# A hybrid decoder layer on one core: another order of work ahead of the decode units, and a first up tile made from x times the gains of the norm

## The reference

```python
h = rms_norm(x, norm1_g) * (1 + scale1) + shift1       # shifts, scales, gates: silu(c) @ w_ada, per sequence
x_lru, g_lru, q_lat, kv_lat, k_rope = split(h @ w_in)
lru_out = rg_lru(causal_dwconv(x_lru)) * gelu(g_lru)   # scan over the tokens
q = rms_norm(q_lat) @ w_uq                             # 8 heads, 64 + 32 wide; norms per head, rotation
attn = attend(q, rms_norm(kv_lat), rotated k_rope)     # keys and values are kv_lat @ w_ukv
x = x + gate1 * (concat(rms_norm(lru_out), rms_norm(attn)) @ w_o)
h2 = rms_norm(x, norm2_g) * (1 + scale2) + shift2
val, gt = split(causal_dwconv(h2 @ w_up), 2)           # width 3, 2 x 2816 columns
x = x + gate2 * ((gelu(gt) * val) @ w_down)
```

## Time and profile before

| | |
|---|---|
| median of 3 runs | 946.93 us (945.82 to 947.53) |
| the profiled execution | 949.23 us, its span 947.4 us |
| PE busy | 919.8 us, 97% of the span, 7805 matmuls |
| DVE, ACT, POOL busy | 637.4, 513.1, 184.3 us |
| chain that ended last | PE 88%, DVE 6%, ACT 2%, DMA 2% |
| DMA | 106 GB/s in the mean |
| longest waits of PE | 5.7 us for x_sample, 3.2 for w_ada, 2.4 for normed_low (L2392), 1.6 for xT |
| PE in front of stored_columns | 1.0 us, for ACT's copy of the fourth stored row (L1620) |

### The profile page before, as it was taken

How to read it: one execution, slowest core, us unless ns; L and a number is a source line. 1 busy time by engine, 2 the same in 40 slices (tenths; PEclk the granted TensorE clock), 3 DMA queues, 4 the chain that set the end, 5 groups by cost and what they waited for, 6 DMA issues and landing times.

```text
span 947.4 us, 20112 instructions
## 1 busy us (share of the span) xinstructions
PE 919.8 (97%) x7805; PEld 858.7 (91%) x7805; DVE 637.4 (67%) x1241; ACT 513.1 (54%) x1147; POOL 184.3 (19%) x163
## 2 busy tenths in 40 slices
PE   5899999999999999999999989999999999999998
PEld 3588876799999999999899979999999999999997
DVE  2893378488888888888863667777777777722321
ACT  2414845689889889898863354444444443311111
POOL 0032323333333324333330301100000001000000
PEclk9999999999999999999998999999999999999999
DMA  9996732300212203202130423333333331653202
GB/s 338 332 281 222 223 134 102 146 2 23 91 59 77 90 24 112 90 24 90 46 91 23 113 60 90 89 89 90 92 96 98 97 97 50 161 153 80 63 1 91
DMA packets 107897, 100.12 MB, mean 106 GB/s; under 512 B 7125, under 2 KB 96597, under 8 KB 105770
## 3 DMA queue, kind: packets, MB, share of 16 engines
q1 hardware_dynamic: 104030, 77.91, 28.1%
q0 software_dynamic: 3456, 20.97, 6.2%
q10 hardware_dynamic: 340, 0.27, 0.1%
HBM read 96.41 MB, written 2.94 MB: 105 GB/s over the span
## 4 chain that ended last, share of the span: by engine, by line
PE 88%; DVE 6%; ACT 2%; DMA 2%; issue 1%; SPq 0%; POOL 0%; DVEq 0%; ACTq 0%; POOLq 0%
PE ps L890 51%; PE ps L1286 20%; PE ps L885 6%; PE ps L1247 2%; PE ps L1183 2%; PE ps L923 2%; DMA RW<-w_ada 2%; PE ps L1062 1%; PE ps L896 1%; PE ps L1282 1%; DVE RB L1996 1%; PE ps L1209 1%; DVE input_low L1929 1%; DVE up_weights_low L2371 0%; DVE small L1970 0%
## 5 line engine op out<-in xcount | busy, mean ns | idle before, releaser
L890 PE MATMUL ps<-normed_high,up_weights_high 128*128 128x260 f32 x704 | 142.5, 284 | 2.5 <-DVE normed_low L2392 2.4
L890 PE MATMUL ps<-normed_high,up_weights_low 128*128 128x260 f32 x704 | 142.5, 284 | 0.0
L890 PE MATMUL ps<-normed_low,up_weights_high 128*128 128x260 f32 x704 | 142.1, 284 | 0.0
L1791 ACT ACTIVATE up_weights_high<-RW 128x1024 fp32r<-128x1024 f32 x44 | 46.6, 1061 | 128.0 <-PE ps L890 128.0
L836 POOL TENSOR_TENSOR latents_low<-RB,latents_high 128x512 fp32r<-128x512 f32 x64 | 82.7, 1292 | 165.7 <-ACT latents_high L1667 165.6
L1286 PE MATMUL ps<-key_weights_high,latents_high 128*128 128x260 f32 x512 | 113.3, 302 | 0.1
L890 PEld LDWEIGHTS ps<-normed_high,up_weights_high 128*128 128x128 f32 x704 | 108.9, 189 | 3.1 <-issue 2.2
L890 PEld LDWEIGHTS ps<-normed_high,up_weights_low 128*128 128x128 f32 x704 | 109.1, 189 | 0.0
L890 PEld LDWEIGHTS ps<-normed_low,up_weights_high 128*128 128x128 f32 x704 | 108.7, 189 | 0.0
L1286 PE MATMUL ps<-key_weights_high,latents_low 128*128 128x260 f32 x512 | 103.1, 283 | 0.0
L1286 PE MATMUL ps<-key_weights_low,latents_high 128*128 128x260 f32 x512 | 103.1, 283 | 0.0
(11 more groups left out here) (350 smaller groups left out, 2069.5 us busy)
## 6 DMA issues: line engine op xcount, KB each, us to landing
RW<-w_ada SPq DMA_DIRECT2D x24, 1024.0 KB, 7.0
RW<-w_up SPq DMA_DIRECT2D x44, 512.0 KB, 5.1
RW<-w_down SPq DMA_DIRECT2D x8, 1408.0 KB, 7.3
RW<-w_in SPq DMA_DIRECT2D x11, 512.0 KB, 6.4
RB<-w_o SPq DMA_DIRECT2D x8, 512.0 KB, 4.2
RB<-x_prompt SPq DMA_DIRECT2D x2, 1024.0 KB, 12.2
o_y_p<-RB SPq DMA_DIRECT2D x4, 448.0 KB
cst<-consts SPq DMA_DIRECT2D x1, 844.5 KB, 12.0
```

The lines of the kernel that those rows point to most:

```text
L890: last = mm(ps[j % 4][rows[0]:rows[1], h, 0:H], lhsT, src[:, h * H:(h + 1) * H], start=start, stop=stop)
L1791: A(wuH[:, KT * g:KT * g + KT, :], wup[:, c, KT * g:KT * g + KT, :], ACT.Copy).then_inc(s_whi, 1)
```

## The change

Stage A. Both orders of jobs change. GELU's tile w_in(11) moves ahead of queries(3). The product with GELU's result and the modulation's last rows move ahead of query tile 3 in DVE's stream, and the modulation's last columns behind it. The recurrent norm (squares, sum, root, lru_normed, split_queries) moves ahead. POOL makes the low key weights and issues the gathers of step 1 behind its additions. Seven calls of `keep_busy` go.

Stage B. The first two up tiles, (0, 0) and (0, 1), are made from x times gains, without root and shift: the decode columns in the same way, and 12 more columns hold the shifts themselves, so that the products give W'(g x) and W'shift. Behind the product DVE multiplies by the root and ACT adds the shift. The tiles from (1, 0) on use h2 as before, which now goes through a ring of five tiles. The sum of the norm stands inside the first tile's products. The state of the convolution is fetched ahead of the last tiles and turned before tile 6 of the output projection.

```diff
@@ jobs
-               "q2", "q3", "w11", "kv0", "kv1"])
-PREP_ORDER = [("c5", 3), ("qst", 3), ("kv2", 1), ("qa", 3), ("kv3", 2), ("spread", 0), ("l0", 3), ("l1", 0), ("l2", 3), ("l3", 0),
-              ("nlru", 1), ("l4", 3), ("l5", 0), ("l6", 3)]
+               "q2", "w11", "q3", "kv0", "kv1"])
+PREP_ORDER = [("c5", 3), ("qst", 3), ("nlru", 3), ("kv2", 1), ("qa", 3), ("kv3", 2), ("spread", 0), ("l0", 3), ("l1", 0),
+              ("l2", 3), ("l3", 0), ("l4", 3), ("l5", 0), ("l6", 3)]
-J_N2, J_FST = job(9), job(10)
+J_N2, J_FST = job(19), job(15)
...
+XW = T + 12
+XH = XW // 2
+HR = 5
@@ sync
-            full(sp, J_WO[KT - 1])
             sp.dma_start(fs_tok, t["state_ffn_conv"].rearrange("l b r (m c) -> (l r m) b c", c=P)).then_inc(s_fst, 16)
@@ gpsimd
-            full(pool, J_WIN[7])
-            nc.gpsimd.memset(QBD[:, :, :, :], 0.0).then_inc(s_bdz, 1)
+            pool.wait_ge(s_kw, 2)
+            for e in range(2):
+                nc.gpsimd.tensor_tensor(kwL[:, e, :, 0:4 * NOPE], wkn[:, :].rearrange("p (g n) -> p g n", g=2),
+                                        kwH[:, e, :, 0:4 * NOPE].bitcast(F32), ALU.subtract).then_inc(s_kw, 1)
...
-            for n in range(2):
-                cached_keys(n, n)
-                cached_latents(n, n)
-
+            cached_keys(0, 0)
+            cached_latents(0, 0)
+            nc.gpsimd.memset(QBD[:, :, :, :], 0.0).then_inc(s_bdz, 1)
             for k in range(1, LT):
...
+            cached_keys(1, 1)
+            cached_latents(1, 1)
@@ tensor, stage A
             queries(2)
-            queries(3)
             w_in(11)
             later_chunk(15)
+            queries(3)
             pe.wait_ge(s_kvn, 1)
             keys_and_values(0)
...
+            claim(pe, J_NLRU)
+            pe.wait_ge(s_lrn, LT - 1)
+            both(J_NLRU, ones, lru_sq[:, 0, :], True, True).then_inc(psum_full[J_NLRU % 4], 1)
             keys_and_values(2)
...
-            keep_busy(spare, 3)
             pe.wait_ge(s_kr, 2)
-            for a in range(4):
+            for a in range(5):
                 stored_rows(a)
-                keep_busy(spare, 1)
-            claim(pe, J_NLRU)
...
@@ tensor, stage B
             for m in range(4, KT):
+                if m == 6:
+                    claim(pe, J_FST)
+                    pe.wait_ge(s_fst, 16)
...
-            keep_busy(flat(j)[:, 768:1024], 4)
...
+            def first_products(g, k):
+                j = up_job(g)
+                for n, (w, x) in enumerate(((wuH, x_high[k]), (wuH, x_low[k]), (wuL, x_high[k]))):
+                    for h in range(2):
+                        last = mm(ps[j % 4][:, h, 0:XH], w[:, KT * g + k, :], x[:, h * XH:(h + 1) * XH],
+                                  start=(k == 0 and n == 0), stop=(k == KT - 1 and n == 2))
...
+            for k in range(KT):
+                pe.wait_ge(s_xlo, k + 1)
+                if k in (0, 4, KT - 1):
+                    pe.wait_ge(s_xs, 1 + (0, 4, KT - 1).index(k))
+                first_products(0, k)
+                if k == 1:
+                    claim(pe, J_N2)
+                    pe.wait_ge(s_nsum, KT - 2)
+                    both(J_N2, ones, sq[:, 0, :], True, False)
+                if k == 2:
+                    pe.wait_ge(s_sq, 2 * KT + 12)
+                    both(J_N2, ones, sq[:, KT - 1, :], False, True).then_inc(psum_full[J_N2 % 4], 1)
...
@@ scalar
+            prep_squares(J_Q[3], query_sq, HEADS * QK)
+            act.wait_ge(s_lrud, 2)
+            lru_squares(0)
+            prep_rstd(4, 2 * HEADS)
+            lru_squares(2)
             key_squares(0)
             key_squares(1)
-            act.wait_ge(s_lrud, 2)
-            lru_squares(0)
             prep_rstd(5, HEADS)
-            lru_squares(2)
             prep_rstd(6, HEADS)
+            rstd(J_NLRU, LW).then_inc(s_rs, 1)
...
+                A(x_high[k][:, 0:NP], xT[:, k, 0:NP], ACT.Identity, bias=small[:, 1:2], scale=gmod[:, k, 0:1]).then_inc(s_xhi, 1)
...
+                if k < KT - 1:
+                    act.wait_ge(s_xused, k + 1)
+                else:
+                    full(act, up_job(1))
+                A(hH[:, k, :], h2[:, k % HR, :], ACT.Identity, bias=modT[:, 3 * KT + k, 0:1]).then_inc(s_h, 1)
@@ vector, stage A
             mod_columns(4)
-            for a in range(2, 4):
-                prep_sums(1 + a, query_sq, HEADS)
-                prep_query_tile(a)
+            prep_sums(3, query_sq, HEADS)
+            prep_query_tile(2)
+            mod_rows(5)
+            dve.wait_ge(s_g, 1)
+            V.tensor_tensor(GG[:, :, :], TA[:, :, :], GG[:, :, :], MUL).then_inc(s_lrud, 1)
+            prep_sums(4, query_sq, HEADS)
+            prep_query_tile(3)
...
-            mod_rows(5)
             mod_columns(5)
-            dve.wait_ge(s_g, 1)
-            V.tensor_tensor(GG[:, :, :], TA[:, :, :], GG[:, :, :], MUL).then_inc(s_lrud, 1)
             full(dve, J_QST)
...
             key_sums(2)
+            dve.wait_ge(psum_free[J_QA % 4], free_value(J_QA))
+            split_queries(0)
+            dve.wait_ge(s_rs, 5)
+            lru_normed()
             full(dve, J_SPREAD)
@@ vector, stage B
+            def gained_low(k):
+                dve.wait_ge(s_xhi, k + 1)
+                V.scalar_tensor_tensor(x_low[k][:, 0:NP], xT[:, k, 0:NP], gmod[:, k, 0:1], x_high[k][:, 0:NP].bitcast(F32), MUL, SUB).then_inc(s_xlo, 1)
+            def gained_samples(a, b):
...
             for m in range(KT):
                 residual(J_WO[m], m, 2 * KT, s_x1, m + 1)
                 if m + 4 < KT:
                     out_low(m + 4)
+                if m > 0:
+                    gained_low(m - 1)
                 if m == 4:
+                    gained_samples(0, 4)
                     up_low(0, 0, 1)
                     up_low(0, 1, 2)
+                if m == 5:
+                    full(dve, J_FST)
...
+                if m == 6:
+                    gained_samples(4, KT - 1)
+            gained_samples(KT - 1, KT)
+            gained_low(KT - 1)
...
+            for k in range(HR):
+                scaled_samples(k)
+                scaled(k)
+                if k == 2:
+                    first_scaled(0)
+                    up_low(1, 0, 3)
+            for k in range(KT):
+                normed_low(k)
+                if 0 < k <= KT - HR:
+                    dve.wait_ge(s_hlo, KT + k)
+                    scaled_samples(k - 1 + HR)
+                    scaled(k - 1 + HR)
+            first_scaled(1)
```

More of the change, by code:

```diff
@@ L261 @@
 J_WO = [job(n) for n in (0, 1, 2, 11, 4, 5, 6, 8)]
-J_N2, J_FST = job(9), job(10)
[L263 to L268, removed]
-def up_job(n):
-    return job(UP0 + n)
+J_N2, J_FST = job(19), job(15)
+BY_MLP = [n + m for n, m in zip(USED, (3, 2, 2, 5))]
+def up_job(n):
+    slot = (n + 1) % 4
+    return slot + 4 * (BY_MLP[slot] + n // 4)
+DOWN0 = 2 * FT
+J_FT = up_job(DOWN0 + 2)
+J_DOWN = [up_job(DOWN0 + m + (m >= 2)) for m in range(KT)]
+J_Y = [up_job(DOWN0 + KT + n) for n in (1, 2, 3, 5)]
+J_YL, J_YS = up_job(DOWN0 + KT + 4), up_job(DOWN0 + KT + 6)
+XW = T + 12
+XH = XW // 2
+HR = 5
 def build(nc, t):
@@ L549, in build @@
         s_x1 = sem("x1_done")
+        s_xhi = sem("gained_high")
+        s_xlo = sem("gained_low")
+        s_xs = sem("gained_samples")
+        s_xused = sem("gained_used")
+        s_first = sem("first_up_scaled")
         s_wup = [sem(f"w_up_in{e}") for e in range(2)]
@@ L1377, in _ @@
             for m in range(4, KT):
+                if m == 6:
+                    claim(pe, J_FST)
+                    pe.wait_ge(s_fst, 16)
+                    for b in range(NS):
+                        c = 512 * (b // 4) + 4 * FT * (b % 4)
+                        last = tr(flat(J_FST)[:, c:c + 4 * FT], fs_tok[:, b, :], 4 * FT)
+                    last.then_inc(psum_full[J_FST % 4], 1)
                 claim(pe, J_WO[m])
@@ L1381, in _ @@
                     out_products(m, k)
-            claim(pe, J_N2)
-            pe.wait_ge(s_nsum, KT - 2)
-            both(J_N2, ones, sq[:, 0, :], True, False)
-            pe.wait_ge(s_sq, 2 * KT + 12)
-            both(J_N2, ones, sq[:, KT - 1, :], False, True).then_inc(psum_full[J_N2 % 4], 1)
-            j = J_FST
-            claim(pe, j)
-            keep_busy(flat(j)[:, 768:1024], 4)
-            pe.wait_ge(s_fst, 16)
-            for b in range(NS):
-                c = 512 * (b // 4) + 4 * FT * (b % 4)
-                last = tr(flat(j)[:, c:c + 4 * FT], fs_tok[:, b, :], 4 * FT)
-            last.then_inc(psum_full[j % 4], 1)
             def up_products(e, g, k):
@@ L1641, in _ @@
                 stored_rows(a)
-            rstd(J_NLRU, LW).then_inc(s_rs, 1)
             stored_rows(4)
@@ L1832, in mlp @@
                     down_high(0)
-                evacuate(m, i, e, 1)
+                first_evacuate(1) if isinstance(i, int) and m == 0 else evacuate(m, i, e, 1)
                 if left >= 2:
@@ L1841, in _ @@
             up_high(1, 0, 1, up_job(0))
-            evacuate(0, 0, 0, 0)
```

(26 more changed lines are left out.)

133 lines of the change are left out of this document (73 added, 60 removed).

## The result

| | before | after |
|---|---|---|
| median | 947.53 us (5 runs, 945.82 to 949.82) | 954.42 us (5 runs, 953.00 to 956.69) |
| ratio, 95% interval | | 1.0075 [1.0057, 1.0093] |
| the profiled execution | 949.23 us, span 947.4 | 956.69 us, span 954.9 |
| queries(2) to unit 0 | 144.78 to 182.19: 37.4 us | 145.39 to 191.09: 45.7 us |
| unit 0 to the copy that waits for up tile five (ACT, L1791 before, L1826 after) | 182.19 to 584.43: 402.2 us | 191.09 to 591.98: 400.9 us |

The loss is 7.1 us by the ratio, predicted were 3.3 with a range that ended at 953.5. By the profiles it is +8.3 in stage A and -1.35 in stage B, and 0.6 us that lie ahead of queries(2). Behind the fifth up tile the two traces run alike (363.0 and 362.9 us to the end).

What follows compares the result with a forecast made beforehand. TensorE, busy 97% of the span, was taken as the bound. Stage A +5.3 (order +3.1, clock +1.0 and +1.2) and stage B -2.0 gave +3.3 us: 950.2 us from a median of 946.93, range 944.5 to 953.5.

Steps and rivals of the forecast that it cites:

- steps 1 to 6: Ahead of unit 0: the new queue order makes TensorE wait 6.3 us for J_QST's slot; unit 0 at 185.3, +3.1 us.
- Step 7: Ahead of unit 0: TensorE's clock falls twice, 3.4 us at 1.2 GHz each, costing +1.0 and +1.2 us.
- The upper bound: Stage A, ahead of the decode units: at most +7 us, around a forecast of +5.3.
- Stage B (-2.0): Entrance of the MLP: 4.6 us won at the second up tile, of which 2.0 remain by tile five.
- the open 10.6 us: Entrance of the MLP before the change: first two up tiles ended at 567.1 instead of 556.5; 1.7 of it clock.
- the idle row: Sign of being right: TensorE idle some 5 to 6 us in front of the turning of the sample queries.
- the clock: Sign of being right: TensorE's granted clock at 0.5 after the idle row ahead of the units.
- the last residual: Sign of being right, at the MLP's entrance: VectorE's last residual ready near 551.
- Unit 0 "near 186 to 188": Sign of being right: the first decode unit starts near 186 to 188.
- draw: Rival, 25%: port waits and second clock fall stay out; A +2, B -3, total 946 to 948.8.
- Faster: Rival, 15%: VectorE reaches mod_columns(5) before TensorE wants J_QST; no 6.3 us wait, A -3.2, B -2, about 941.7.
- The last one: Rival, 5%: state's DMA lands past 536.5 and clock falls in first up tile; B +0.5, A as forecast, 953.

Runs made afterwards that it cites:

- all fillers: Changed kernel plus 13, 3 and 4 filler calls in TensorE's three idle stretches ahead of the units: 952.71 us, ratio 1.0047 against the kernel before.
- experiment 5: Stage B's diff with state copies on ScalarE, ratio 0.9992; kernel before repeated unedited, 0.9980; kernel before plus four filler calls at the MLP's entrance, 0.9997.
- experiment 6: Changed kernel with stage A's queues reordered and state copies on ScalarE: ratio 1.0001; the same with four filler calls between stored rows: 0.9999.
- stage B alone: Only the diff's stage B parts, put on the kernel before: 947.20 us, ratio 1.0001.
- stage A alone: Only the diff's stage A parts, put on the kernel before: 956.09 us, ratio 1.0102.
- additions held back: Changed kernel with GpSimd's additions of the recurrent squares held until VectorE's last query tile is done: 952.84 us, one run.
- columns copied early: Changed kernel with VectorE copying the modulation's last columns right behind the product with GELU's result, ahead of the last query tile: 954.43 us, ratio 1.0073.

## Why the prediction was right in its order and wrong in its size

**Stage A, steps 1 to 6 (order, +3.1): right.** The wait was predicted as 6.3 us up to 166.9; measured are 6.13 up to 167.45, of which 0.6 lie ahead of queries(2). Slot, port waits (2.3 predicted, 2.0 measured) and VectorE's order were the cause; with the clock held up the order costs 3.5 us. The wait in front of the second stored row, 177.7 less the norm's end in my working, is there with 1.89 us.

**Step 7 (clock, +1.0 and +1.2): this step failed.** I took the length that the trace of before shows at both stages, 3.4 us at 1.2 GHz, for each of the two falls. Measured are 10.2 and 6.8 us, and 4.8 us of time instead of 2.2: 2.8 for the first fall instead of 1.0, 1.95 for the second instead of 1.2. Nor did VectorE hide 0.7 us of the first, as the step has it. In the timelines of DVE, the changed kernel first and the one with all fillers behind it, VectorE itself waits for J_QA:

```profile
176.69 0.27 DVE L2219 COPY QA<-ps 128x64 f32<-128x64 f32 x1 [4.45 <-PE ps L1156]
```
```profile
174.62 0.28 DVE L2223 COPY QA<-ps 128x64 f32<-128x64 f32 x1 [1.83 <-PE ps L1158]
```

The upper bound ("+7" for the whole stage, measured +8.3) rested on the same length, although the idle stretch in front was ten times that of before (6.13 against 0.60 us). The trace of before held a longer fall, the 6.8 us near 500 (0.66 in the stretch of experiment 5). Half of that for each of two falls gives 3.1 + 3.4 + 3.4 = +9.9 as an estimate of the upper bound, and that would have held. Why one fall is long and another short, no run here shows. The Trainium skill (TensorE: Matmul & The Clock Gate, "HAM oscillation — how this bites in real kernels") names waits between bursts as what throttles the array again. The first fall, in 6.13 us of idle, agrees. The second came with a wait of 1.89 us and thin rows, the kernel before without fillers fell for 10.2 us behind waits of 0.60 and 0.32 us, and experiment 6 shows that equal waits needn't give equal falls: that the rule would give both falls, as the prediction has it, isn't borne out as it stands there.

**Stage B (-2.0): right in its steps, smaller at its end.** Less the 8.9 us of stage A, with the prediction behind it: the state's wait 1.46 (1.5), the factor 554.8 (554.4), the second tile 562.85 (562.5), the start of tile four 570.8 behind the low weights (570.5), its end 576.9 (576.4). The gain of 1.85 us at tile four is 1.35 at tile five. The wait for low weights of 0.17 us in front of tile five is a part of that; the rest I can't name. That 1.7 of the open 10.6 us were the clock was wrong: with and without that fall the first five tiles take the same time. In the ratio stage B alone shows +0.1 us, -0.9 to +1.2; its profile's -1.2 lies just outside, while two equal kernels came out 0.9 us apart by their medians and 0.2% by the ratio. Whether it is worth 1 us or nothing stays open.

**The sum.** +3.5 + 4.8 - 1.35 = +6.95 us by the profiles, with the 0.6 us ahead of queries(2) the 7.5 by which the spans differ; +7.1 by the ratio. That they meet so closely is in part luck, since the ratios of stage A alone (9.7 us) and of the kernel with all fillers (4.5 us, where the profiles leave 3.5 - 1.35) are 2 us and more off the profiles' sums. Of the signs, the idle row, the clock, the last residual (560.2, less 8.9: 551.3) and the low weights came. Unit 0 "near 186 to 188" didn't, it was 191.09: the clock again. Of the rivals, "draw" wanted neither port waits nor a second fall: both are there. "Faster" hung on a start of the sample queries before 163.8: it was 167.45. The last one wanted the state's DMA past 536.5 and a fall in the first tile: the clock is at 1.0 there.

## What to carry to other kernels

When a step moves forward in one engine's queue, write down what it overtakes and which PSUM slot that work frees: here a product that waits for GELU passed four small steps, and TensorE, which shares their slot, stood for 6 us. Taking the named wait away only moved it to the next job of the slot; the whole group had to move. As an upper bound, price an idle stretch of TensorE as idle time plus all that follows at 1.2 GHz until dense work returns, not by the shortest fall that the old trace happens to show. Here filling the idle stretch alone gained 1.1 us in the profile, filling the thin stretches behind it too gained 4.8 (2.7 by the ratios). And one profile shows one draw of the falls: compare the lengths of a stage only beside the clock of the same profiles, and take the verdict from many runs.

## What the runs showed of the chip that I hadn't expected

- Stretches at 1.2 GHz ahead of the units were 3.4, 6.8 or 10.2 us long. With 6.1 us of idle they were of 10.2 us (changed kernel, stage A alone), with 5.1 and 6.6 us of 6.8 (additions held back, columns copied early); without any long idle stretch, in the thin rows of the kernel before without fillers, again of 10.2.
- They aren't a property of the program alone. The same instructions ahead of the units gave one fall of 3.4 us or two of 6.8 (A 37.6 or 42.0, on two chips), and one or two of 3.4 on one chip. A fall of 6.8 us late in the attention (it starts between 496 and 505), worth 3.25 us in the kernel before, was in 9 of the 17 profiles, and one of 3.4 us in one more. How much of the scatter between runs this makes isn't shown. Over the 29 runs of the kernel before on the last experiments' chip, mean granted clock and time go together with a correlation of -0.66, under half of the variance.
- One GpSimd addition of 128x520 held up not only VectorE's operations with two SBUF inputs but a plain copy of 32x512 too: 1.53 us beside an addition that began at 164.53, instead of 0.50.
